# Recurrent gate products of one kernel: one float32 product each, or three products of rounded parts

## The reference, cut to what matters

```python
xc = causal_dwconv(xb, lru_conv_w) + lru_conv_b
xh = x.reshape(b_, s_, H_B, DB)
r = jax.nn.sigmoid(jnp.einsum("bshi,hij->bshj", xh, w_a) + b_a)
i = jax.nn.sigmoid(jnp.einsum("bshi,hij->bshj", xh, w_x) + b_x)
log_a = -LRU_C * r * jax.nn.softplus(-lam)
a = jnp.exp(log_a)
u = x * i * jnp.sqrt(-jnp.expm1(2.0 * log_a))
```

## Time and profile before

| | us |
|---|---|
| median of three runs | 3364.1 (3363.22 to 3364.41) |
| the profiled execution, time | 3363.22 |
| the profiled execution, span of its instructions | 3361.4 |
| TensorE busy | 3344.8 |
| VectorE busy | 2080.3 |
| ScalarE busy | 1610.0 |
| GpSimd busy | 168.9 |

### The profile page before, as it was taken

The page is one execution under the profiler, slowest core; times in us unless marked ns, Lnnn a source line. Parts: engine busy times, 40 slices in busy tenths (PEclk is TensorE's granted clock), DMA queues, the critical chain, the costliest instruction groups (busy, mean ns, idle before and its releaser), DMA issues.

```text
span 3361.4 us, 43843 instructions
## 1 busy us (share of the span) xinstructions
PE 3344.8 (100%) x17548; PEld 2867.5 (85%) x17548; DVE 2080.3 (62%) x2839; ACT 1610.0 (48%) x2160; POOL 168.9 (5%) x233
## 2 busy tenths in 40 slices
PE   9999999999999999999999999999999999999999
PEld 7899888899899888899988888888888887788887
DVE  5567555656767655656667555655555666657564
ACT  5543444445543444434555454444445444455543
POOL 2000000000000000000000000000000321200000
PEclk9999999999999999999999999999999999999999
DMA  8665665565555566565566565555556555566555
GB/s 266 211 195 167 187 178 174 190 186 170 182 178 175 176 182 181 173 202 170 176 197 219 180 189 180 155 163 172 174 177 186 167 168 165 169 211 189 174 182 169
DMA packets 313516, 613.91 MB, mean 183 GB/s; under 512 B 20792, under 2 KB 22628, under 8 KB 313184
## 3 DMA queue, kind: packets, MB, share of 16 engines
q1 hardware_dynamic: 301520, 581.05, 56.5%
q0 software_dynamic: 9520, 23.75, 2.3%
q10 hardware_dynamic: 2272, 6.30, 0.5%
HBM read 604.43 MB, written 6.59 MB: 182 GB/s over the span
## 4 chain that ended last, share of the span: by engine, by line
PE 96%; DVE 2%; ACT 1%; issue 0%; DMA 0%; POOL 0%; SPq 0%; DVEq 0%; ACTq 0%
PE acc L1471 29%; PE acc L1473 29%; PE acc L1472 29%; PE tr L1524 2%; PE tr L1577 2%; PE nm L1619 1%; DVE work L1061 1%; DVE weights_lo L1057 1%; PE sc L1595 1%; PE tr L1608 0%; PE sc L1585 0%; ACT work L842 0%; ACT weights_hi L831 0%; PE nm L1595 0%; PE sc L1599 0%
## 5 line engine op out<-in xcount | busy, mean ns | idle before, releaser
L1057 DVE TENSOR_TENSOR weights_lo<-weights_raw,weights_hi 128x1024 fp32r<-128x1024 f32 x1104 | 1345.7, 1229 | 1029.2 <-ACT weights_hi L831 1025.0
L831 ACT ACTIVATE weights_hi<-weights_raw 128x1024 fp32r<-128x1024 f32 x1104 | 1163.2, 1059 | 1228.4 <-PE acc L1473 1130.9
L1471 PE MATMUL acc<-weights_hi,u_hi 128*128 128x512 f32 x2368 | 942.0, 398 | 2.0 <-DVE weights_lo L1057 1.9
L1473 PE MATMUL acc<-weights_hi,u_lo 128*128 128x512 f32 x2368 | 923.9, 390 | 0.0
L1472 PE MATMUL acc<-weights_lo,u_hi 128*128 128x512 f32 x2368 | 922.8, 390 | 0.0
L1471 PEld LDWEIGHTS acc<-weights_hi,u_hi 128*128 128x128 f32 x2368 | 444.9, 188 | 98.8 <-issue 8.7
L1473 PEld LDWEIGHTS acc<-weights_hi,u_lo 128*128 128x128 f32 x2368 | 444.5, 188 | 94.0
L1472 PEld LDWEIGHTS acc<-weights_lo,u_hi 128*128 128x128 f32 x2368 | 445.2, 188 | 88.1
L1471 PE MATMUL acc<-weights_hi,y_hi 128*128 128x512 f32 x1280 | 504.7, 394 | 3.8 <-DVE y_lo L1061 2.6
L1473 PE MATMUL acc<-weights_hi,y_lo 128*128 128x512 f32 x1280 | 499.3, 390 | 0.0
L1472 PE MATMUL acc<-weights_lo,y_hi 128*128 128x512 f32 x1280 | 498.9, 390 | 0.0
(11 more groups left out here) (254 smaller groups left out, 1995.6 us busy)
## 6 DMA issues: line engine op xcount, KB each, us to landing
weights_raw<-in_w_in_dram SPq DMA_DIRECT2D x384, 512.0 KB, 3.8
weights_raw<-in_w_out_dram SPq DMA_DIRECT2D x256, 512.0 KB, 4.1
weights_raw<-in_a_w_in_dram SPq DMA_DIRECT2D x176, 512.0 KB, 4.0
weights_raw<-in_b_w_in_dram SPq DMA_DIRECT2D x112, 512.0 KB, 3.8
weights_raw<-in_c_w_in_dram SPq DMA_DIRECT2D x112, 512.0 KB, 4.0
weights_raw<-in_w_mem_kv_dram SPq DMA_DIRECT2D x64, 512.0 KB, 4.6
kv_scratch<-work ACTq DMA_DIRECT2D x8, 512.0 KB, 4.5
qk_tiles<-in_w_a_dram POOLq DMA_DIRECT2D x8, 512.0 KB, 4.3
```

The lines of the kernel that those rows point to most:

```text
L831: SC_E.activation(WH[:, b % RING], RAW[:, b % RING], ACT.Copy).then_inc(sem("hi_done"), 1)
L1057: V.tensor_tensor(WL[:, b % RING], RAW[:, b % RING], WH[:, b % RING].bitcast(F32), ALU.subtract).then_inc(sem("lo_done"), 1)
L1471: T.matmul(dst, hi_l, hi_r, start=start, stop=False, **kw)
L1473: return T.matmul(dst, lo_l, hi_r, start=False, stop=stop, **kw)
```

## The change

The float32 product of lgate becomes split3, three products of rounded parts, as in the weight stream. Two new pieces make the parts. The piece wax (one for each of the two gates w, in slots e-2 and e-1) has ACT write the rounded weights WXH[w] and DVE the rest, WXL[w]. The piece cvs (in slot e+3 for p = 1 to 3, and e+6 for p = 0, so one slot ahead of the first lgate) has ACT write the rounded features CVH and DVE the rest, CVL. No buffer is added: WXH lies over the q tiles of the chunkwise recurrence, WXL over WAX itself, CVH over ZT and CVL over ZB, and some waits are added or moved for these overlaps.

```diff
@@ lru_in(p)
             c = pl.here() + 1
             if p == 0:
                 c += 3
+            s = pl.here() - NB
+            for w in range(2):
+                pl.piece(s + 6 + w, "wax", w=w)
+            pl.piece(c + 2, "cvs")
             for w in range(2):
                 pl.piece(c + 3 + w, "lgate", l=l, p=p, w=w)
@@ views
         WAX = view(QKB, 2048, 2, 4, 256)
+        WXH, WXL = view(QKR, 0, 2, 4, 256), view(QKR, 2048, 2, 4, 256)
+        CVH, CVL = view(WR, 12560, 4, 256), view(WR, 8464, 4, 256)
@@ POOL
                     elif k == "load_fg":
-                        wait(pool, "ms_pe", p.last["ms"])
+                        wait(pool, "lw_pe", p.last["lgate"])
@@ ACT
+                    elif k == "wax":
+                        act.wait_ge(sem("wax_in"), 32 * (p.n // 2 + 1))
+                        wait(act, "ms_pe", last["ms"])
+                        wait(act, "lw_pe", last.get("lgate"))
+                        SC_E.activation(WXH[:, p.w], WAX[:, p.w], ACT.Copy).then_inc(sem("wx_hi"), 1)
+                    elif k == "cvs":
+                        wait(act, "cx_c", last["cx"])
+                        wait(act, "yb_lo", last.get("lry"))
+                        if p.n == 0:
+                            act.wait_ge(sem("tb_st"), 16)
+                        SC_E.activation(CVH, CV, ACT.Copy).then_inc(sem("cv_hi"), 1)
@@ ACT, lrz
-                        if p.n == 0:
-                            act.wait_ge(sem("tb_st"), 16)
+                        wait(act, "lw_pe", last["lgate"])
@@ DVE, zb
                         dve.wait_ge(sem("mm_done"), done(p))
+                        wait(dve, "lw_pe", last["lgate"])
@@ DVE
+                    elif k == "wax":
+                        wait(dve, "wx_hi", p)
+                        V.tensor_tensor(WXL[:, p.w], WAX[:, p.w], WXH[:, p.w].bitcast(F32), ALU.subtract
+                                        ).then_inc(sem("wx_lo"), 1)
+                    elif k == "cvs":
+                        wait(dve, "cv_hi", p)
+                        V.tensor_tensor(CVL, CV, CVH.bitcast(F32), ALU.subtract).then_inc(sem("cv_lo"), 1)
@@ PE
                     elif k == "lgate":
-                        wait(pe, "cx_c", last["cx"])
-                        pe.wait_ge(sem("wax_in"), 32 * (p.n // 2 + 1))
+                        wait(pe, "cv_lo", last["cvs"])
+                        wait(pe, "wx_lo", p)
                         for f in range(4):
                             h, jt = f // 2, f % 2
                             for it in range(2):
-                                m = T.matmul(TR[:, h, 256 * jt:256 * jt + 256], WAX[:, p.w, 2 * h + it, jt * P:jt * P + P],
-                                             CV[:, 2 * h + it], start=it == 0, stop=it == 1)
+                                i, js = 2 * h + it, slice(jt * P, jt * P + P)
+                                m = split3(TR[:, h, 256 * jt:256 * jt + 256], WXH[:, p.w, i, js], WXL[:, p.w, i, js],
+                                           CVH[:, i], CVL[:, i], it == 0, it == 1)
```

More of the change, by code:

```diff
@@ L503, in program @@
         SM = sb("smalls", [P, 256])
+        with nc.sbuf_tensor("qk_rounded", [P, 4096], F32R) as QKR:
+            with nc.sbuf_tensor("work_rounded", [P, 13824], F32R) as WR:
+                pass
         QKB = sb("qk_tiles", [P, 4096])
```

## The result

The changed kernel takes 3388.1 us (median of 5 runs, 3385.7 to 3390.1) against 3364.0 for the kernel before (5 runs, 3363.2 to 3364.4): ratio 1.0071 with the interval 1.0059 to 1.0082, so 0.7% slower. The forecast was 3381, with a range to 3388, so the measured time stands at the range's upper end. The waits that it walked through came true nearly row by row, and one of its rivals came true on top.

The account below looks back on a forecast made before the run. PE was taken to bound the kernel. Waits of 4.62 + 1.18 + 3.73 + 3.78 = 13.3 us a layer, 26.6 in both, minus 9.2 gained gave +17.4: 3381 us (3380.6 or 3381.5), range 3371 to 3388.

Parts of the forecast that it names:

- one of its rivals: Clock falls: half clock behind the 3.7 us waits in groups 2 and 3, 7 us or twice that, 3388 to 3395; chance 0.12.
- What bounds the kernel: PE, busy 3344.8 of 3361.4 us: each microsecond leaving its queue is gained in full, each waited is lost in full.
- PE's own work: 16 lgate groups: eight float32 products in 3.45 us become 24 rounded ones in 2.88 us, -9.2 us in all.
- Weights, group 0: ACT's first wax waits 7.9 us for the late transfer, delaying DVE's splits; PE waits 4.62 us a layer.
- Features, group 1: PE's first lgate waits 1.08 us for CVL behind the convolution, 1.18 us with the pipeline refill, per layer.
- Groups 2 and 3: Two wax subtractions on DVE delay the convolution, so PE waits for CVL: 3.73 and 3.78 us per layer with refill.
- The sum: Waits of 13.3 us a layer, 26.6 in both, less 9.2 gained: +17.4 us, so 3380.6 us.
- Edits at nothing: Waits of zb and lrz for the last lgate, load_fg issued later, lru's start moving with the second lgate: no cost.

Follow-up runs that it names:

- experiment 5: Experiment 4's kernel with the second wax piece of groups 1 to 3 moved from slot e-1 to e+4, behind the convolution: 3361.6 us, ratio 0.9993.
- experiment 7: The changed kernel with all copies and subtractions, but PE makes float32 products of unrounded values and doesn't wait for the copies: 3379.9 us, ratio 1.0048.
- experiment 3: The changed kernel with group 0 alone altered: wax pieces in slots e+4 and e+5, lgates and what follows two slots later: 3379.1 us, ratio 1.0047.
- Experiment 1: The changed kernel with eight float32 products of constants filling PE's wait before the first lgate of groups 2 and 3: 3380.5 us, ratio 1.0050.
- experiment 2: The changed kernel with lgate pieces of groups 1 to 3 and the recurrence behind them one slot later, cvs unmoved: 3375.7 us, ratio 1.0036.
- experiment 4: The changed kernel with the alterations of experiment 2 and experiment 3 together: 3366.2 us, ratio 1.0007.
- experiment 8: Experiment 7's kernel, but PE waits for the subtractions as in the changed kernel, still making float32 products: 3400.0 us, ratio 1.0107.
- experiment 9: Experiment 4's kernel with the two wax subtractions moved from DVE to GpSimd, in the same slots: 3393.3 us, ratio 1.0085.

## Why the prediction was right, and which step failed

- **What bounds the kernel.** Right. PE was at its limit, so every wait was paid in full. The means of DVE and ACT (62% and 48%) said nothing of the places where they are full, as experiments 5 and 7 show.
- **PE's own work**, -9.2. Measured 2.82 us a group, not 2.88: about 0.63 x 16 = 10.1 us. The row of the long stretch carried over within 2%.
- **Weights, group 0**, 4.62 a layer. DVE's two rows were forecast within 0.1 us. The lgate moved by 632.49 - 626.77 = 5.72, where 626.77 is the start of its first matmul before; less 1.10, exactly 4.62. The walk needed the queue on both engines, the landing time of the transfer and the 0.96 and 1.14 us spacings; experiment 3 got the cost back (9.0 for two layers).
- **Features, group 1**, 1.18 with the refill. The view has 0.99 (0.98 in layer 1), counted from the end of the last product before it. The next would have started 0.16 earlier (rows at 817.50: 0.12 us step, 0.28 us long), so PE lost 1.15, and some 0.1 at the restart.
- **Groups 2 and 3**, 3.73 and 3.78. The view has 3.56 and 3.55, in layer 1 3.56 twice; with the same 0.16, 3.72 each and the restart. Slot e+1's idle time and the two subtractions ahead of the convolution were as said.
- **The sum**, 3380.6. This is the step that failed: it put the clock at nothing, and the long waits slow what follows them, by 6.8 us. Experiment 1 takes that away, keeps the rest, and measures 3380.5. That this is so near is partly luck: the products gave back 0.9 us more than forecast, the waits took 0.8 more, and the start of that execution 0.6 more than in the one before. The text had the mechanism as a rival, with nearly the right price (1.7 us a time, 7 in all; measured 1.5 three times and 2.3), and the measured time stands at the end of the range only because the range had been stretched for a part of it. It gave the rival 0.12 with the argument that these were single waits in a full stream. That argument was no evidence: the row at the program's start showed the low clock behind an idle stretch of 2.56 us, and no row of the kernel before showed full clock behind a stretch as long. The Trainium skill, "TensorE: Matmul & The Clock Gate", section HAM oscillation, says that a gap of this kind brings the half clock back at each occurrence, and the trace agrees, four times out of four.
- **Budget.** Waits for splits 11.1 - 3.0 = 8.1, lgate waits 16.2, and 0.21 for each of the 15 new waits that the view doesn't count (in group 0 the lgate moved by 4.62 while the four rows sum to 3.79), 3.1; clock 6.8, program start 1.1, products -10.1: 25.2 us, against 3388.4 - 3363.2 = 25.2 in the two profiled executions.
- **Edits at nothing.** PE waits for nothing in the changed kernel that it didn't wait for before, beside the splits and the features, so they were nothing.

In the experiments the failed step was another: "a slot later frees a slot" (experiments 2 and 4) held the producer fixed while its own queue moved along with it.

## What to carry to other kernels

Price an added producer step by walking the queues of the engines that do it, at the place where it stands: a copy hung in front of its own data, or two subtractions ahead of a convolution, cost far more than their 1 us each, and moving them is worth more than the product gain (10 us here against 27 us recovered by experiment 5). When the walk ends in a PE wait of several microseconds, price the products behind it at half clock too, unless the trace shows full clock behind a wait as long. Before you give DVE's overflow to an idle GpSimd, measure how long DVE's own instructions take meanwhile.

## What the runs showed of the hardware

- **Clock.** Each of the twelve idle stretches of PE of 3.54 to 3.74 us before an lgate (four each in the changed kernel and experiments 3 and 8) was followed by products at the 1.2 GHz level. In the changed kernel this level began 0.3 us after the restart in group 2 of layer 0 and some 1 us after it in two others, and there the slow steps lasted 3.4 us; behind the fourth wait the first product was slow already, and they lasted 5.1 us. In experiment 9 four waits of 2.55 and 2.56 us, each with one of 0.7 us some 6 us ahead of it, had the low level behind them too. Its row for 860 to 890 us shows the same 0.94 as that of the changed kernel, where the wait was 3.55 us:

```profile
860.00:890.00 30.00, 26.52 (x204) 25.77 (x202) 25.81 (x31) 13.15 (x16) 6.05 (x2) 0.94 0.56 171
```

  In experiments 2, 4, 5 and 7 waits for the features of 0.57 to 1.72 us left the mean clock at 1.000, and filled waits did too.
- **GpSimd beside DVE.** A subtraction of 128x1024 takes GpSimd 2.7 us (median of 16, 2.4 to 3.4) and DVE 1.23 us, and while both work on such operands DVE's take 3.1 us. ACT's copies stayed at 1.05 us. The Trainium skill, "GPSIMD Engine Reference", section 1 (Specifications), lists the interface as shared with VectorE, with contention for instructions that read two operands; the trace agrees, and gives the price: beside two subtractions of GpSimd, DVE's instructions with two operands take 3.9 us longer in group 1 and 4.1 in group 0.
- **Float32 products.** Eight take 3.46 us and the 24 rounded ones 2.82, each with its own weights: three rounded products cost 0.35 us where one float32 product costs 0.43. The 3.46 us hold the step behind the group: before, in group 0, the next product starts 3.27 us after the first float32 one (626.77 to 630.04), and the one behind it 0.42 us later instead of 0.23.
